# Hybrid decoder step: the recurrent stage reordered over ACT, DVE and POOL, and the first output tiles of both mixers computed in one pass

## The reference

```python
def c_mixer(h, conv_buf, h0, w_in, conv_w, conv_b, w_rg, b_rg, w_ig, b_ig, lam, w_out):
    gate, xr = jnp.split(h @ w_in, 2, axis=-1)
    xc, new_buf = causal_dwconv(xr, conv_buf, conv_w)
    xc = xc + conv_b
    hs, h_last = rglru(xc, h0, w_rg, b_rg, w_ig, b_ig, lam)
    y = (jax.nn.gelu(gate) * hs) @ w_out
...
    r = jax.nn.sigmoid(jnp.einsum('btnc,ncd->btnd', xb, w_rg).reshape(bsz, t, D_RNN) + b_rg)
    i = jax.nn.sigmoid(jnp.einsum('btnc,ncd->btnd', xb, w_ig).reshape(bsz, t, D_RNN) + b_ig)
    log_a = -LRU_C * r.astype(jnp.float32) * jax.nn.softplus(-lam.astype(jnp.float32))
    a = jnp.exp(log_a)
    u = jnp.sqrt(-jnp.expm1(2.0 * log_a)) * (i * xc).astype(jnp.float32)
    # hc = a * hc + u, token by token
```

## Time and profile before

| what | value |
|---|---|
| median of 3 runs | 2239.72 us (2236.7 to 2239.73) |
| profiled execution: time, span | 2239.78 us, 2238.1 us |
| busy: PE, DVE, ACT, POOL | 2153.4, 1134.4, 700.5, 85.6 us |
| mean granted clock of PE | 0.968 of full speed |
| recurrent stage, from `xr4` to the end of `out67.0` | 1627.86 to 1755.15 us |

### The profile page before, as it was taken

The page is one execution under the profiler, slowest core; times in us unless marked ns, Lnnn a source line. Parts: engine busy times, 40 slices in busy tenths (PEclk is TensorE's granted clock), DMA queues, the critical chain, the costliest instruction groups (busy, mean ns, idle before and its releaser), DMA issues.

```text
span 2238.1 us, 37961 instructions
## 1 busy us (share of the span) xinstructions
PE 2153.4 (96%) x17060; PEld 2095.8 (94%) x17060; DVE 1134.4 (51%) x1534; ACT 700.5 (31%) x914; POOL 85.6 (4%) x101
## 2 busy tenths in 40 slices
PE   8999999999999999999998999999997899999998
PEld 7999999897869899999987999999897899999998
DVE  6443244755545744234567443244798664423466
ACT  4222222322233432122344222122455432212243
POOL 2000000111020000000000000000013000000000
PEclk9999999997979999999999999999999999999999
DMA  4222222232131222222212222222222222222222
GB/s 164 89 82 97 92 95 76 97 114 76 57 115 57 76 95 90 87 107 90 81 67 94 90 85 95 90 95 76 76 84 71 76 95 89 86 91 95 95 86 76
DMA packets 33489, 198.57 MB, mean 89 GB/s; under 512 B 4504, under 2 KB 4792, under 8 KB 15408
## 3 DMA queue, kind: packets, MB, share of 16 engines
q1 hardware_dynamic: 29376, 183.87, 23.3%
q0 software_dynamic: 3952, 12.28, 1.8%
HBM read 191.68 MB, written 4.46 MB: 88 GB/s over the span
## 4 chain that ended last, share of the span: by engine, by line
PE 83%; DVE 12%; ACT 2%; issue 2%; DMA 1%; SPq 0%; ACTq 0%; DVEq 0%
PE acc L1536 63%; PE acc L1639 12%; DVE w_lo L969 2%; PE acc L1575 2%; PE acc L1847 1%; PE acc L1773 1%; DVE t L1067 1%; DVE act_lo L1080 1%; DVE xsum L1089 1%; ACT w_hi L641 1%; PE acc L1610 1%; PE acc L1728 1%; PE acc L1813 1%; DVE xi L1450 1%; DVE x L1074 1%
## 5 line engine op out<-in xcount | busy, mean ns | idle before, releaser
L1536 PE MATMUL acc<-act_hi,w_hi 128*128 128x260 f32 x3072 | 620.3, 283 | 3.6 <-DVE gu L1168 3.6
L1536 PE MATMUL acc<-act_hi,w_lo 128*128 128x260 f32 x3072 | 618.7, 283 | 0.0
L1536 PE MATMUL acc<-act_lo,w_hi 128*128 128x260 f32 x3072 | 618.2, 283 | 0.0
L1536 PEld LDWEIGHTS acc<-act_hi,w_hi 128*128 128x128 f32 x3072 | 474.0, 188 | 6.3 <-DVE gu L1168 3.8
L1536 PEld LDWEIGHTS acc<-act_hi,w_lo 128*128 128x128 f32 x3072 | 473.5, 188 | 0.4
L1536 PEld LDWEIGHTS acc<-act_lo,w_hi 128*128 128x128 f32 x3072 | 472.9, 188 | 0.5
L969 DVE TENSOR_TENSOR w_lo<-raw,w_hi 128x2048 fp32r<-128x2048 f32 (+3 forms) x179 | 389.7, 2177 | 43.7 <-ACT w_hi L641 43.7
L641 ACT ACTIVATE w_hi<-raw 128x2048 fp32r<-128x2048 f32 (+3 forms) x179 | 323.7, 1808 | 281.0 <-DMA raw<-in_weights 280.9
L1168 DVE TENSOR_TENSOR gu<-acc,rs_pre 128x520 f32<-128x520 f32 x164 | 114.5, 699 | 447.7 <-PE acc L1536 447.6
L1536 PE MATMUL acc<-hid_hi,w_hi 128*128 128x260 f32 x1024 | 206.3, 283 | 0.2
L1536 PE MATMUL acc<-hid_hi,w_lo 128*128 128x260 f32 x1024 | 206.0, 282 | 0.0
(11 more groups left out here) (265 smaller groups left out, 2255.0 us busy)
## 6 DMA issues: line engine op xcount, KB each, us to landing
raw<-in_weights SPq DMA_DIRECT2D x138, 1024.0 KB, 4.8
raw<-in_weights SPq DMA_DIRECT2D x32, 896.0 KB, 4.6
ring<-in_k_pages POOLq DMA_DIRECT2D x16, 256.0 KB, 3.2
ring<-in_v_pages POOLq DMA_DIRECT2D x16, 256.0 KB, 3.2
raw<-in_weights SPq DMA_DIRECT2D x12, 256.0 KB, 6.9
x<-in_x SPq DMA_DIRECT2D x8, 260.0 KB, 7.4
out_y<-x SPq DMA_DIRECT2D x8, 260.0 KB, 2.0
raw<-in_weights SPq DMA_DIRECT2D x4, 512.0 KB, 3.4
```

The lines of the kernel that those rows point to most:

```text
L1536: ins = nc.tensor.matmul(a[0:width, half, 0:HALF], w[slot][:, at:at + width], m[:, half * HALF:(half + 1) * HALF], start=first and n == 0, ...
```

## The change

- `old_taps` sums the three older taps of the sample tokens for all chunks once, on DVE, in the first feed-forward block; in the stage one addition of 8 columns per chunk is left of three multiply-adds.
- The newest tap with the bias goes from DVE to ACT (`base`).
- The low parts `xc_lo` and the products with the roots go from POOL to DVE (`conv_lo`, `driven`).
- `c_steps` is rewritten: on ACT `conv` of chunks c+2 and c+3 now stands ahead of `gates` of c and c+1 (it stood behind), and on DVE each `xr` or `gt` drain is followed by one `conv` and `lo` (two drains stood side by side). Six roots are taken ahead of `gates(6)` and six scans start there; the other two follow.
- The last states are copied to `h_tail` by ACT, and stored from there.
- `mixer_out`, for both mixers, works on `out0`, `out1` and `out23.0` together, chunk by chunk. Unit `out4` is split earlier (after `gt7`, and after the last head in attention), `out2` after `gt6`.

```diff
+        pl.early[pl.unit[f"{s}.out4"]] = f"{s}.pv{HEADS - 1}"
...
-        for unit, job in (("xr6", "xr4"), ("gt2", "xr6"), ("gt4", "gt2"), ("gt6", "gt4")):
+        out_pairs(s, ("c_w_out", 0))
+        for unit, job in (("xr6", "xr4"), ("gt2", "xr6"), ("gt4", "gt2"), ("gt6", "gt4"), ("out2", "gt6"),
+                          ("out4", "gt7")):
             pl.early[pl.unit[f"{s}.{unit}"]] = f"{s}.{job}"
-        out_pairs(s, ("c_w_out", 0))
...
-                    for c in range(KC):
-
-                        pool.wait_ge(xch_ready, c + 1)
-                        nc.gpsimd.tensor_tensor(xc_lo[:, c % 4, :], xi[:, c, :], xc_hi[:, c % 4, :].bitcast(F32),
-                                                ALU.subtract).then_inc(xcl_ready, 1)
                     pool.wait_ge(tail_ready, KC)
...
+                def base(c):
+
+                    if c < 4:
+                        wait_first(act, s, c)
+                        act.wait_ge(t_ready, x_count(s, 1, KC - 1))
+                    else:
+                        wait_drained(act, f"{s}.xr{c}")
+                    nc.scalar.activation(xi[:, c, :], lru_v[:, c, :], ACT.Identity, scale=par("convc_w", 3 * KC + c),
+                                         bias=par("convc_b", c)).then_inc(base_ready, 1)
+
...
-                for c in range(4):
+                gelu(0)
+                gelu(1)
+                done(f"{s}.gt6")
+                for c in range(2, 6):
+                    mixed_hi(c - 2)
                     gelu(c)
                 done(f"{s}.gt7")
-                for c in range(4, KC):
...
+                act.wait_ge(hs_ready, KC + 2)
+                nc.scalar.activation(h_tail[:, :, :], xi[:, :, SEQ - 1:TOK], ACT.Copy).then_inc(h_kept, 1)
                 out_squares(s)
...
+                chained(nc.vector.tensor_tensor(state[:, :, 0, :], state[:, :, 0, :], w(0), ALU.mult))
+                for j in range(1, CC - 1):
+                    chained(nc.vector.tensor_tensor(product, state[:, :, j, :], w(j), ALU.mult))
+                    chained(nc.vector.tensor_tensor(state[:, :, 0, :], state[:, :, 0, :], product, ALU.add))
+
             def ffn(s):
                 for j in range(HID[0]):
                     hidden(s, j)
+                    if s == 0 and j == 6:
+                        old_taps()
...
-                    chained(nc.vector.tensor_scalar(out, u, w(CC - 1), par("convc_b", c), ALU.mult, ALU.add))
+                    dve.wait_ge(base_ready, c + 1)
+                    chained(nc.vector.tensor_tensor(out[:, SEQ:TOK], out[:, SEQ:TOK],
+                                                    par("state_c", c * (CC - 1) * DEC, DEC), ALU.add))
...
-                        chained(nc.vector.scalar_tensor_tensor(out=out[:, SEQ:TOK], in0=st(j), scalar=w(j),
-                                                               in1=out[:, SEQ:TOK], op0=ALU.mult, op1=ALU.add))
...
+                def conv_lo(c):
+
+                    dve.wait_ge(xch_ready, c + 1)
+                    nc.vector.tensor_tensor(xc_lo[:, c % 4, :], xi[:, c, :], xc_hi[:, c % 4, :].bitcast(F32),
+                                            ALU.subtract).then_inc(xcl_ready, 1)
...
+                    dve.wait_ge(root_ready, c + 1)
+                    dve.wait_ge(xi_ready, c + 1)
+                    nc.vector.tensor_tensor(lru_v[:, c, :], lru_v[:, c, :], xi[:, c, :], ALU.mult).then_inc(u_ready, 1)
+
+                def scan(c):
+
+                    dve.wait_ge(u_ready, c + 1)
+                    nc.vector.tensor_tensor_scan(xi[:, c, 0:SEQ], lru_a[:, c, 0:SEQ], lru_v[:, c, 0:SEQ], 0.0,
+                                                 ALU.mult, ALU.add).then_inc(hs_ready, 1)
...
+                last_gate(6)
+                driven(6)
+                scan(6)
+                mixed(0)
+                mixed(1)
+                mixed_lo(0)
+                done(f"{s}.gt6")
+                mixed(2)
+                mixed_lo(1)
+                last_gate(7)
+                driven(7)
+                scan(7)
+                decode_rows(EARLY_SCANS, KC)
+                for c in range(3, KC):
+                    mixed(c)
+                    mixed_lo(c - 1)
+                    if c == 4:
+                        done(f"{s}.gt7")
                 mixed_lo(KC - 1)
-
-                dve.wait_ge(stored, 16 * 8)
+                dve.wait_ge(h_kept, 1)
                 outputs(s)
...
-                k_outer([J[f"{s}.out{m}"] for m in range(2)], [U[f"{s}.out0"]], inp,
-                        lambda c: pe.wait_ge(mixh_ready, n0 + list(chunks).index(c) + 1),
-                        lambda c: pe.wait_ge(mixl_ready, n0 + list(chunks).index(c) + 1), chunks)
-                last_pairs(s, inp)
+                n = U[f"{s}.out0"]
+                first, second, third = (claim(J[f"{s}.{name}"]) for name in ("out0", "out1", LAST_PAIRS[0] + ".0"))
+                wait_unit(n)
+                wait_unit(n + 1)
+
...
+                for i, c in enumerate(chunks):
+                    hi, lo = inp(c)
+                    pe.wait_ge(mixh_ready, n0 + i + 1)
+                    product(c, w_hi, hi, i == 0, False)
+                    product(c, w_lo, hi, False, False)
+                    pe.wait_ge(mixl_ready, n0 + i + 1)
+                    product(c, w_hi, lo, False, i == KC - 1)
+                last_pairs(s, inp, 1)
...

+        return [*pair("conv", 0), *pair("lo", 0),
+                ("xr", 4), ("conv", 2), ("lo", 2), ("xr", 5), ("conv", 3), ("lo", 3), *pair("gates", 0),
...
+    return [*pair("base", 0), ("conv", 0), ("base", 2), ("conv", 1), ("xr", 4), ("base", 3), ("conv", 2), ("conv", 3),
...
```

More of the change, by code:

```diff
@@ L613, in _ @@
                     store(ccstate_o, state[:, :, DEC:(CC - 1) * DEC])
[L614 to L621, removed]
+                    pool.wait_ge(h_kept, 1)
+                    store(h_o, h_tail[:, :, :])
                     pool.wait_ge(stored, count[0])
@@ L897, in gates, with roots @@
                     nc.scalar.activation(a2[:, :], lru_a[:, c, :], ACT.Square).then_inc(a2_ready, 1)
+                def roots(chunks):
+                    for c in chunks:
+                        act.wait_ge(v_ready, c + 1)
+                        nc.scalar.activation(lru_v[:, c, :], lru_v[:, c, :], ACT.Sqrt, scale=0.25).then_inc(root_ready, 1)
                 act.wait_ge(nl_made, 1)
                 for kind, c in c_steps("scalar"):
-                    if kind == "conv":
+                    if kind == "base":
+                        base(c)
+                    elif kind == "conv":
                         conv_hi(c)
@@ L905, in recurrent @@
                         done(f"{s}.i{c}")
+                    elif kind == "roots":
+                        roots(range(c))
                     else:
                         done(f"{s}.{kind}{c}")
-                for c in range(KC):
-                    act.wait_ge(v_ready, c + 1)
-                    nc.scalar.activation(lru_v[:, c, :], lru_v[:, c, :], ACT.Sqrt, scale=0.25).then_inc(root_ready, 1)
+                roots(range(EARLY_SCANS, KC))
                 def gelu(c):
@@ L1473, in recurrent @@
                         done(f"{s}.i{c}")
+                    elif kind == "scan":
+                        driven(c)
+                        scan(c)
                     else:
@@ L1647, in last_pairs @@
                     for i, pair in enumerate(LAST_PAIRS):
+                        if half == 0 and i < begun:
+                            continue
                         half_pair(f"{s}.{pair}.{half}", n + i, half, inp,
@@ L1706, in mixer_out, with product @@
             def mixer_out(s, n0, chunks=range(KC), inp=act_in):
-                k_outer([J[f"{s}.out{m}"] for m in range(2)], [U[f"{s}.out0"]], inp,
-                        lambda c: pe.wait_ge(mixh_ready, n0 + list(chunks).index(c) + 1),
-                        lambda c: pe.wait_ge(mixl_ready, n0 + list(chunks).index(c) + 1), chunks)
-                last_pairs(s, inp)
+                n = U[f"{s}.out0"]
+                first, second, third = (claim(J[f"{s}.{name}"]) for name in ("out0", "out1", LAST_PAIRS[0] + ".0"))
+                wait_unit(n)
+                wait_unit(n + 1)
+                def product(c, w, part, start, stop):
+                    low_tile, high_tile = slice(2 * c * P, (2 * c + 1) * P), slice((2 * c + 1) * P, (2 * c + 2) * P)
+                    for a, at in ((first, low_tile), (second, high_tile)):
+                        for half in range(2):
+                            ins = nc.tensor.matmul(a[:, half, 0:HALF], w[n % SLOTS][:, at], cols(part, half),
+                                                   start=start, stop=stop)
+                        if stop:
+                            ins.then_inc(acc_ready, 1)
+                    for i, at in enumerate((low_tile, high_tile)):
+                        ins = nc.tensor.matmul(third[:, i, 0:HALF], w[(n + 1) % SLOTS][:, at], cols(part, 0),
```

(5 more changed lines are left out.)

62 lines of the change are left out of this document (36 added, 26 removed).

## The result

The changed kernel takes 2249.3 us (median of 6 runs), the kernel before 2239.1 (6 runs): a ratio of 1.0049, 95% interval 1.0038 to 1.006. It is 10.2 us slower. The forecast was 2248.8, "slower" at 0.78. The profiled execution of the changed kernel is the slowest of its six, 2251.02 us; its span is 2249.3.

The account below looks back on a forecast made before the run. PE was taken as the bound, busy 2153.4 of 2238.1 us, so its waits count. Recurrent stage 2.6, attention 2.7 and clock 3.7 sum to 9.0 on 2239.78: 2248.8 us, range 2243 to 2254.5.

Parts of the forecast that it names:

- The circle of waits: Recurrent rounds: r's tanh waits for convolutions on DVE, delaying PE; xr6 +4.9 us, next rounds 19.0 against 15.87.
- The output tiles: Recurrent tail: PE starts them at 1724.3 against 1708.43, +15.9 us, and takes 18.6 instead of 29.33.
- wait for chunk 4: Recurrent output tiles: PE waits 1.4 us for chunk 4, behind the split of out4.
- The gain: Recurrent tail: output tiles take 18.6 instead of 29.33 us; idle 4.24 before out45.0 goes through out4's early split.
- The late unit: Both stages: out6 needs out0's slot, fetched only when out1 is done; 3.5 us idle before each out67.0.
- Clock: PE at half clock after new idle times: 1.5 us at each out67.0, 0.7 at the output tiles, +3.7 in all.
- The sum: Whole kernel: recurrent stage 2.6, attention 2.7, clock 3.7, together 9.0 us slower, 2248.8 us.
- The rivals: Circle doesn't close, 2232.9 us (chance 0.10); tail wins back rounds' loss, 2243.7 (0.12); PE half clock through rounds, 2270 (0.04).
- the circle doesn't close: Rival, recurrent rounds: ACT reaches the tanh before the copies, rounds take 14.3 us, total 2232.9; chance 0.10.

Follow-up runs that it names:

- gates_first: Changed kernel, only reordered on ACT and DVE: gates of c, c+1 ahead of copies and low parts of c+2, c+3, drains ahead of convolutions; 2233.43 us.
- two_acc_attention: Changed kernel with the attention stage's output by two accumulators again, two tiles first and half pairs behind; 2244.07 us, ratio 1.0025 to the kernel before.
- changed_again: The changed kernel itself, unaltered, measured and profiled again on another chip; 2248.68 us, ratio 1.0044 to the kernel before.
- two_acc_both: Changed kernel with two accumulators in both the attention and the recurrent stage's output; 2242.45 us, ratio 1.0018 to the kernel before.
- scan_in_gap: On gates_first plus two accumulators in both stages: chunk 3's product and scan moved between gates of chunks 6 and 7 on DVE; 2223.3 us.

## Why the prediction was right, step by step

- **The circle of waits**: right, shown by gates_first. Rounds 19.10 and 19.03 for 19.0. Counted from the restart in the block ahead (1603.69 before, 1608.62 after), `xr6` starts 5.0 us later (4.9 forecast), `gt2` 8.2 (8.0), `gt4` 11.3 (11.1), `gt6` 11.5 (11.2): it starts at 1707.82, so that its round is 15.8, as forecast.
- **The output tiles**: 16.3 us later, for 15.9. Three tiles in 18.69 us for 18.6, and here the reason given was wrong. No wait for chunk 4 is in the trace; what exceeds the 17.2 of 144 matmuls is half clock: the first 12 take 2.74 us, from 1729.67 to the row of 1732.41, instead of 1.43. I had kept 0.7 for that and 1.4 for the wait, 2.1 in all for what took 1.5.

```profile
1731.97 0.64 PE L1795 MATMUL acc<-xc_hi,w_lo 128*128 128x260 f32 x2
1732.41 0.76 PE L1790 MATMUL acc<-xc_lo,w_hi 128*128 128x260 f32 x4
```

- **The gain**: `out45.0` without a wait, right; the early split is worth 3.0 us by itself.
- **The late unit** `out6`: right, shown by two_acc_attention in the attention stage. Idle times forecast 3.5; in attention 3.11 and 3.18, in the recurrent stage 4.33 and 3.02, as the landing fell.
- **Clock**: 1.5 us at each forecast. In attention 16 matmuls at 0.217 instead of 0.119 lose 1.6. In the recurrent stage the tile takes 7.75 instead of 5.72, 2.0 lost, and 8.58 in changed_again (1756.54 to 1765.12), 2.9 lost. The term was right in attention and too small by 0.5 and 1.4 here.
- **The sum**: attention 2.7 + 1.5 = 4.2 forecast, 4.1 and 4.3 measured. Recurrent 2.6 + 1.5 + 0.7 = 4.8 forecast, 6.5 and 5.8 measured in two profiles. Of the 1.7 more in the first, 0.4 is the later start of the output tiles, 0.8 the landing and 0.5 the clock behind it; 0.6 went the other way in the three tiles, and the rest lies in small pieces. The profiled spans differ by 11.2; 1.3 of it came up in the first 30 us, where ACT waited for a weight, and was still there at the idle time in the feed-forward block ahead of attention (402.55 against 401.24). changed_again has it too (402.52), but two_acc_attention and two_acc_both, which are the same program up to there, `old_taps` and all, reached that point at 400.47 and 399.97, so it is spread and not a cost of the change.
- **Luck**: the mechanisms are shown, but that forecast and median lie 0.5 us apart is in part chance. The change costs 10.2 us by the medians where the sum had 9.0, and 0.7 of the difference is hidden because the forecast was counted from a profiled execution of 2239.78, above the median of 2239.1 of all six runs. Within the sum, a wait that did not occur stands against clock that was put too low.
- **The rivals**: none happened. That the circle doesn't close is what gates_first made true by hand: forecast at 14.3 us a round, 15.8 for the last, and a time of 2232.9; it runs at 14.34, 14.42 and 15.87, and takes 2233.43.

## What to carry to other kernels

Two engines that hand work to and fro are not bound by the sum of work on either but by the longest chain through both. Moving an operation ahead of another that PE waits for can lengthen it although DVE got less to do and ACT hardly more (708.7 us against 700.5); walk the circle before believing the busy shares. Here the order cost 16 us of stage and hid what the cheaper convolution, the early split and the early scans had won (5.1, 3.0 and 3.7 us of stage).

Working on more tiles at once lets more work run as inputs arrive, but it also keeps weights in their slots longer: ask which transfer waits for that slot. And in one profile most of a gain of 1.84 us ahead of a wait was lost in PE's clock behind it (scan_in_gap); measure a stage between two fixed points of the trace before judging by medians.

## What the hardware showed that I had not expected

After an idle time of 3.11 us PE ran 1.1 us at full clock, then 3.4 us at half, then full again. A fall of the clock must be looked for behind the restart too, not only at it. Nor is it the same each time, or in step with the idle time: behind 4.33 us idle it lasted 4.9 us, behind 3.02 us at the same place 6.2. And behind equal idle times of 3.7 us in the same place (the feed-forward block ahead of attention), full speed was there at once in changed_again (402.52 to 402.86) and after 6.0 us in the changed kernel (402.55 to 408.54).
